# A two-block model forward pass on one core: the first modulation by feature halves, with two of its blocks on TensorE

## What is computed

```
mod = c @ ada_w[l] + ada_b[l]
sh1, sc1, gt1, sh2, sc2, gt2 = [m[:, None, :] for m in jnp.split(mod, 6, axis=-1)]

h = rmsnorm(x, norm1_g[l]) * (1.0 + sc1) + sh1
p = h @ w_in[l]
xr, yr, q, k, v, ga, gb = jnp.split(p, cuts, axis=-1)
...
q = head_rmsnorm(q.reshape(b_, s_, ATT_HEADS, HEAD_DIM), q_norm_g[l])
k = head_rmsnorm(k.reshape(b_, s_, ATT_HEADS, HEAD_DIM), k_norm_g[l])
y_b = stick_breaking_attention(q, k, v)
mix = jax.nn.sigmoid(ga) * y_a + jax.nn.sigmoid(gb) * y_b
x = x + gt1 * (mix @ w_out[l])
```

## Time and profile before

| | us |
|---|---|
| median of 3 runs | 1700.46 (1700.05 to 1700.58) |
| the profiled execution | 1701.61 |
| its span, first to last instruction | 1699.8 |
| TensorE busy in the span | 1653.3 (97%) |
| DVE busy | 988.4 (58%) |
| ScalarE busy | 801.5 (47%) |
| GpSimd busy | 790.1 (46%) |

### The profile page before, as it was taken

One profiled execution on the slowest core, in us unless ns is written; L12 is line 12 of the kernel. 1 busy time (PEld: TensorE's weight loads), 2 busy tenths in 40 slices (PEclk: granted clock), 3 DMA queues, 4 the chain that ended last, 5 costly groups with the idle time before them and its releaser, 6 DMA issues.

```text
span 1699.8 us, 19723 instructions
## 1 busy us (share of the span) xinstructions
PE 1653.3 (97%) x7340; PEld 1347.5 (79%) x7340; DVE 988.4 (58%) x1170; ACT 801.5 (47%) x1005; POOL 790.1 (46%) x577
## 2 busy tenths in 40 slices
PE   4999999999999999999999999999999999999997
PEld 2778887878778888888887888888878888888885
DVE  6676787777837817715642767566446554155541
ACT  2565565666434425514342333677653444244442
POOL 1244443543555545554563544455573342543425
PEclk7999999999999999999999999999999999999999
DMA  9333433242233332333322322211222131331312
GB/s 369 124 124 117 132 109 125 89 136 87 80 101 99 95 101 90 99 124 99 98 89 68 112 84 83 72 42 56 75 87 87 51 99 50 99 99 51 99 50 74
DMA packets 46462, 166.89 MB, mean 98 GB/s; under 512 B 5152, under 2 KB 5280, under 8 KB 45856
## 3 DMA queue, kind: packets, MB, share of 16 engines
q1 hardware_dynamic: 46368, 165.63, 29.8%
HBM read 163.52 MB, written 2.10 MB: 97 GB/s over the span
## 4 chain that ended last, share of the span: by engine, by line
PE 93%; DVE 5%; ACT 1%; DMA 1%; issue 1%; POOL 0%; SPq 0%; POOLq 0%; DVEq 0%; ACTq 0%
PE lin L651 17%; PE lin L653 17%; PE lin L652 17%; PE big L651 7%; PE big L653 7%; PE big L652 7%; DVE scr L1585 1%; PE big L757 1%; PE m_o L777 1%; PE big L1067 1%; PE big L1066 1%; PE big L1065 1%; DMA scr<-ada 1%; PE big L770 1%; PE big L768 1%
## 5 line engine op out<-in xcount | busy, mean ns | idle before, releaser
L617 POOL TENSOR_TENSOR w_lo<-raw,w_hi 128x512 fp32r<-128x512 f32 x200 | 284.4, 1422 | 651.8 <-ACT w_hi L1104 651.7
L651 PE MATMUL lin<-h_hi,w_hi 128*128 128x512 f32 x936 | 368.9, 394 | 2.9 <-POOL w_lo L620 1.8
L653 PE MATMUL lin<-h_hi,w_lo 128*128 128x512 f32 x936 | 365.2, 390 | 0.0
L652 PE MATMUL lin<-h_lo,w_hi 128*128 128x512 f32 x936 | 365.0, 390 | 0.0
L620 POOL TENSOR_TENSOR w_lo<-raw,w_hi 128x512 fp32r<-128x512 f32 x209 | 302.1, 1446 | 14.4 <-ACT w_hi L1104 14.4
L1104 ACT ACTIVATE w_hi<-raw 128x1024 fp32r<-128x1024 f32 (+1 forms) x209 | 217.5, 1041 | 159.4 <-PE m_b L669 50.3
L651 PEld LDWEIGHTS lin<-h_hi,w_hi 128*128 128x128 f32 x936 | 176.1, 188 | 40.7 <-POOL w_lo L620 2.2
L653 PEld LDWEIGHTS lin<-h_hi,w_lo 128*128 128x128 f32 x936 | 176.1, 188 | 37.0
L652 PEld LDWEIGHTS lin<-h_lo,w_hi 128*128 128x128 f32 x936 | 176.2, 188 | 36.6 <-issue 0.7
L617 POOL TENSOR_TENSOR qk_hl<-raw,qk_hl 128x512 fp32r<-128x512 f32 x43 | 60.3, 1402 | 144.2 <-ACT qk_hl L1104 144.1
L651 PE MATMUL lin<-y_hi,w_hi 128*128 128x512 f32 x260 | 101.7, 391 | 1.9 <-DVE y_lo L1749 1.9
(11 more groups left out here) (492 smaller groups left out, 3443.0 us busy)
## 6 DMA issues: line engine op xcount, KB each, us to landing
raw<-weights SPq DMA_DIRECT2D x245, 512.0 KB, 3.6
slab<-ada SPq DMA_DIRECT2D x32, 512.0 KB, 4.4
scr<-ada SPq DMA_DIRECT2D x16, 512.0 KB, 6.3
raw<-weights SPq DMA_DIRECT2D x10, 256.0 KB, 2.7
x<-x_t SPq DMA_DIRECT2D x2, 1024.0 KB, 6.4
out_t<-scr SPq DMA_DIRECT2D x8, 256.0 KB, 2.6
raw<-weights SPq DMA_DIRECT2D x4, 448.0 KB, 3.3
rgw<-rg_w SPq DMA_DIRECT2D x1, 1024.0 KB, 6.6
```

The source lines that it names most:

```text
L617: nc.gpsimd.tensor_tensor(lo[:, 0:4 * P], raw[:, s, 0:4 * P], hi[:, 0:4 * P].bitcast(F32), ALU.subtract).then_inc(w_half, 1)
L651: nc.tensor.matmul(psum_of(n), wh, hi(k), start=(k == 0), stop=False)
L652: nc.tensor.matmul(psum_of(n), wh, lo(k), start=False, stop=False)
L653: last = nc.tensor.matmul(psum_of(n), wl, hi(k), start=False, stop=(k == nk - 1))
```

## The change

- **Halves.** The ada matrix of sh1 and sc1 is laid out anew: blocks 0 to 7 hold sh1 and sc1 for the first 512 features (chunks 0 to 3 of h), blocks 8 to 15 those for chunks 4 to 7. DVE accumulates the first half, starts the second (blocks 8, 9), makes chunks 0 to 3 of h, accumulates blocks 10 to 15, and makes chunks 4 to 7.
- **Two blocks on TensorE.** Blocks 0 and 1 (DIRECT) are not accumulated; sixteen one-column products by the columns of c sum them in m_o, between the fifth and the sixth square of x. DVE adds this to the bias before its last block of the first half. All counts of `ada_used` fall by two.
- **PSUM scratch.** The root stays in m_a, and the gained chunks go to big bank 2 and m_b in turn, not to `rstd` and `tmp`.
- **Units side by side.** `pair` becomes `beside`, with a part of the chunks. Chunks 0 to 3 of q0 and k0, then of v0 and q1; `modulation(1)`; chunks 4 to 7 of q0, k0, v0 together, then of q1, then k1. v0 and q1 use big banks 0 and 1. k1 is cut in three around the head squares. q1 and k1 are then done before the scores of head 0.
- **Copies.** ScalarE copies q0, k0, v0, squares q0, copies q1, squares k0, then splits the weights that `split_ahead(q1)` allows (v1, xr0, yr0), and takes the roots after them.
- **Homes and loads.** The weights of q1 and k1 get homes in free rows of y_hi and y_lo. RING now has the ada blocks 0 to 15 in it, between the weights; `diff`, 448 KB of the constants, is loaded with the gate weights. Some semaphores are joined.

The diff, cut to its core:

```diff
@@ ring_plan
         if h == 0:
-            units += [("q", 0, 8), ("k", 0, 8), ("v", 0, 8), ("ada", a, 8), ("ada", a + 1, 8), ("q", 1, 8),
-                      ("ada", a + 2, 8), ("k", 1, 8), ("ada", a + 3, 8), ("v", 1, 8), ("ada", a + 4, 8)]
+            units += [("ada", i, 8) for i in range(10)] + [("q", 0, 8), ("k", 0, 8), ("ada", 10, 8), ("ada", 11, 8)]
+            units += [("v", 0, 8), ("ada", 12, 8), ("ada", 13, 8), ("q", 1, 8), ("ada", 14, 8), ("ada", 15, 8)]
+            units += [("k", 1, 8), ("ada", a, 8), ("v", 1, 8), ("ada", a + 1, 8)]
             continue
...
+        if h == 1:
+            units += [("ada", a - 2, 8), ("ada", a - 1, 8), ("yr", g, 8), ("ada", a, 8), ("ga", g, 8), ("ada", a + 1, 8),
...
@@ home_plan
-    windows = ((("w_out", 3), ("p_out", 6), None), (("a_out", 0), ("rv", 2), ("qn", HEADS - 1)))
+    windows = ((("w_out", 3), ("p_out", 6), None), (("a_out", 0), ("rv", 2), ("qn", HEADS - 1)),
+               (("q", 0), ("v", 1), None))
@@ SP
-                    sp.wait_ge(ada_used, max(j - NA + 1, ADA_FIRST))
+                    sp.wait_ge(ada_used, max(j - NA + 1, ADA_FIRST) - DIRECT)
@@ PE
             for k in range(DK):
                 square(k + 1, k == 0, k == DK - 1)
+                if k == 4:
+                    direct_blocks()
             modulation(0)
-            modulation(1)
...
                 if h == 0:
-                    pair(("q", 0), ("k", 0), H, L, normed(0))
-                elif h < HEADS:
+                    beside((("q", 0), ("k", 0)), H, L, normed(0), range(4))
+                    beside((("v", 0), ("q", 1)), H, L, normed(0), range(4))
+                    modulation(1)
+                    beside((("q", 0), ("k", 0), ("v", 0)), H, L, normed(0), range(4, DK))
+                    unit("q", 1, H, L, part=range(4, DK))
+                    unit("k", 1, H, L, part=range(4))
+                elif 1 < h < HEADS:
                     unit("q", h, H, L)
                 if h == 1:
-                    unit("k", h, H, L)
+                    pe.wait_ge(v_copied, 1)
+                    pe.wait_ge(q_copied, 2)
...
                 if h == 0:
+                    unit("k", 1, H, L, part=range(4, 6))
                     head_square(2, m_b[:])
+                    unit("k", 1, H, L, part=range(6, DK))
@@ ACT
-            norm_root(square_used, 8, D)
-            split_ahead(0)
-            highs(0)
+            norm_root(square_used, 8, D, m_a[:])
+            split_ahead(0, 1)
+            highs(0, range(2))
+            split_ahead(0, 2)
+            highs(0, range(2, 4))
+            split_ahead(0, 4)
+            highs(0, range(4, DK))
+            for u in range(4):
+                act.wait_ge(unit_done, u + 1)
+                to, signal = ((A(S1["q"], 0), q_copied), (A(S1["k"], 0), k_copied), (V1, v_copied),
+                              (A(S1["q"], 1), q_copied))[u]
+                if u == 3:
+                    head_square(1, A(S1["q"], 0))
+                    act.wait_ge(unit_done, UNIT[("q", 1)] + 1)
+                nc.scalar.activation(to, psum_of(u), ACT.Copy).then_inc(signal, 1)
+            head_square(2, A(S1["k"], 0))
...
+                if h == 0:
+                    split_ahead(UNIT[("q", 1)])
@@ DVE
-            for a in range(ADA_FIRST):
-                accumulate(a)
...
+            for half in range(2):
+                cols = slice(4 * half, 4 * half + 4)
+                for a in range(DIRECT, 10) if half == 0 else range(10, ADA_FIRST):
+                    if a == DK - 1:
+                        dve.wait_ge(direct_done, 1)
...
+                    accumulate(a)
+                dve.wait_ge(mod_done, half + 1)
...
+                        v.scalar_tensor_tensor(out=scaled(0, k), in0=x[:, k], scalar=sm(A1 + k), in1=m_a[:],
+                                               op0=M, op1=M).then_inc(pre_h, 1)
```

More of the change, by code:

```diff
@@ L184, in bank_plan @@
             turn[ring] = 0
-        bank[n] = turn[ring] % ring
-        turn[ring] += 1
+        if (kind, j) in (("v", 0), ("q", 1)):
+            bank[n] = 2 if kind == "v" else 3
+        else:
+            bank[n] = turn[ring] % ring
+            turn[ring] += 1
         before[n] = last.get(bank[n])
@@ L713, in modulation, with beside @@
                 last.then_inc(mod_done, 1)
-            def pair(a, b, hi, lo, ready):
-                na, nb = UNIT[a], UNIT[b]
-                for n in (na, nb):
-                    if BEFORE[n] is not None:
+            def beside(units, hi, lo, ready, part=range(DK)):
+                units = [UNIT[u] for u in units]
+                for n in units:
+                    if BEFORE[n] is not None and part[0] == 0:
                         pe.wait_ge(*freed(n))
-                for k in range(DK):
+                for k in part:
                     pe.wait_ge(*ready(k))
-                    for n in (na, nb):
-                        if k == 0:
+                    for n in units:
+                        if k == part[0]:
                             pe.wait_ge(w_split, PACK[n] + 1)
@@ L732, in pair, with direct_blocks @@
                             last.then_inc(unit_done, 1)
+            def direct_blocks():
+                pe.wait_ge(blocks_loaded, 16 * DIRECT)
+                for m in range(DK):
+                    at = 16 + 8 * (m // 4) + m % 4
+                    for b in range(DIRECT):
+                        last = nc.tensor.matmul(m_o[:, at:at + 1], direct[b][:, m // 4, (m % 4) * P:(m % 4 + 1) * P],
+                                                p_("c", b), start=(b == 0), stop=(b == DIRECT - 1))
+                last.then_inc(direct_done, 1)
             def gained(r):
@@ L1174, in gate, with highs @@
                 act.wait_ge(rgate_done, counted(rgate_done))
-            def highs(r):
-                for k in range(DK):
+            def highs(r, part=range(DK)):
+                for k in part:
                     act.wait_ge(pre_h, DK * r + k + 1)
-                    nc.scalar.activation(h_hi[:, k], tmp[:, k % 4], ACT.Identity,
+                    nc.scalar.activation(h_hi[:, k], scaled(r, k), ACT.Identity,
                                          bias=sm(MOD + 24 * r + k)).then_inc(h_high, 1)
@@ L2312 @@
             home_of[:] = blocks(source(kind, j))
-    ada = i["ada_w"][0].reshape(DK, P, 6, D).transpose(1, 2, 0, 3).reshape(P, NADA, 2, T)
+    ada = i["ada_w"][0].reshape(DK, P, 6, D).transpose(1, 2, 0, 3).reshape(P, 6, DK, 2, T)
+    ada[:, 0:2] = ada[:, 0:2].transpose(0, 3, 2, 1, 4).copy()
+    ada = ada.reshape(P, NADA, 2, T)
     params = np.concatenate([
```

136 lines of the change are left out of this document (85 added, 51 removed).

## The result

| | before | after |
|---|---|---|
| median (lowest to highest), 6 runs each on one chip | 1700.52 us (1699.55 to 1701.47) | 1706.02 us (1704.36 to 1707.81) |
| ratio, 95% interval | | 1.0033 (1.0023 to 1.0042) |
| the profiled execution | 1701.61 us | 1704.36 us |
| its span | 1699.8 us | 1702.4 us |

The change makes the kernel 5.5 us slower. The forecast was 1704.7 us, 4.2 us slower, in a range of 1699.9 to 1708.4. The two marks of the forecast lie at 79.54 us (`scores`, 74.26 before) and 95.95 us (`suffixes`, 91.46 before).

A forecast was written before the change was run, and what follows sets the result against it. TensorE, busy 93%, was taken as the bound, decided before 96 us. Behind by 5.2 us at the scores, 7.3 us with the low clock, 4.2 us at the suffixes after givebacks; added to the median: 1704.7 us, range 1699.9 to 1708.4.

The forecast's parts named there:

- The two marks of the forecast: Starts of the first scores and first suffixes on TensorE; the suffixes' shift was taken as the shift of the end.
- Loads and direct blocks: Start of the kernel: first products end at 25.4 us; two blocks off DVE pay about 1 us, not 2.6 us.
- rival A: Start: the direct products let TensorE's clock fall, first half 3.9 us later, restart 2.2 us later, 1706.9 us; chance 0.22.
- First half of h: h_lo 0 to 3 there at 29.3 to 33.3 us; TensorE works from 31.7 to 44.1, 10.9 us of work.
- Second half, the deciding term: DVE's six remaining accumulations beside five half splits take 12.1 us; TensorE restarts at 51.5, 8.7 us later than before.
- The turns: Second half: DVE accumulations and GpSimd half splits alternate, about 1.1 us each, 12.1 us in all; 7.9 us without.
- rival B: Second half: no turns on DVE, restart at 48.4, 4.0 us less than forecast, 1700.7 us; chance 0.14.
- The scores: First scores: uncovered chain through block 16, yr0's load, splits and roots; TensorE stands 8.1 us, scores at 79.4.
- rival C: First scores: yr0's load is no bound, TensorE stands 4.7 us instead of 8.1, 1701.3 us; chance 0.12.
- D: rival B and rival C together: 7.4 us less than forecast, 1697.3 us; chance 0.10.
- The clock at the scores and what is given back: Low clock adds 2.1 us at scores; a 1.76 us wait and 1.7 us low clock go; suffixes 4.2 us later.
- the step that carries the shift to the end: After 96 us: TensorE is busy to 408 us, so the suffixes' shift, 4.2 us, is the shift of the end.

The follow-up runs named there:

- e4: The changed kernel with no direct blocks on TensorE, all sixteen accumulated on DVE; 1704.62 us, ratio to before 1.0032.
- e3: The changed kernel with k1's weights split after the second half of h, not while DVE accumulates; 1703.8 us, ratio to before 1.0028.
- e1: The changed kernel with the load of yr0 issued ahead of ada block 19; 1701.7 us, ratio to before 1.0012.
- e5: The changed kernel with the edits of e2, e3 and e4 together; 1694.94 us, ratio to before 0.997.
- e7: The changed kernel with the edits of e2 and e3, the two direct blocks left on TensorE; 1696.3 us, ratio to before 0.9979.
- e2: The changed kernel with ScalarE's roots of the head norms ahead of the splits of v1, xr0 and yr0; 1697.51 us, ratio to before 0.9983.
- e8: e5 with head squares and v1's split ahead of q1's copy, plus unread matmuls in TensorE's two idle gaps; 1694.2 us, ratio to before 0.9968.
- e10: e9 plus three unread fp32 products in TensorE's first idle gap; 1691.03 us, ratio to before 0.9946.
- e9: e5 with head squares and v1's split ahead of q1's copy, second modulation products before v0 and q1's last chunk; 1693.77 us, ratio to before 0.9964.

## Why the prediction was right, step by step

**Loads and direct blocks.** DVE's first block came at 13.86 (13.8 was said), it waited 0.36 us for the direct products (0.5), those took 3.63 us (3.4) and ended at 20.65 (20.6), the last squares ended at 23.52 (23.7), the products at 25.19 (25.4). The clock did not fall here, as it would have under rival A. The sentence that the two blocks "pay about 1 us" is wrong all the same, in its sign: e4 has its first products 1.65 us earlier without them, and its whole trace from the suffixes up to 440 us 1.4 us earlier. The working compared the end with the two accumulations' 2.6 us of DVE time and not with when DVE would have been done; it had both numbers for that, 1.27 us a block and 1.32 us an accumulation.

**First half of h.** h_lo 0 to 3 were done at 28.64, 30.22, 31.83 and 32.64, each 0.7 us earlier than said: the operations with one operand in PSUM kept 0.75 us beside half splits of 1.28 us. (The pair shown for it in the earlier trace rows overlapped by 0.4 us only; here it is shown in full.) TensorE began at 28.70 and not at 31.7, since q0's matmuls don't wait for k0's split. It made nothing of that (the burst ended at 43.97, 44.1 was said), because k0's split let it go on at 31.08, and the clock was low until 36.

**Second half, the deciding term.** 12.14 us for six accumulations (12.1), restart at 50.37 (51.5). That is the term that decides, and its size is right. The turns are shown by e3 and e4, and rival B, that the accumulations keep 1.29 us, is refuted. The Trainium skill, GPSIMD Engine Reference, Key points, has the rule that decided between the two readings of the earlier trace rows: DVE contends with GpSimd where it has two SBUF inputs, which fits both the 2.2 us of the accumulations and the 0.75 us of the h operations. The rule gives no price there; here it is 0.9 us for each of the two. The restart came 1.1 us sooner than said. The accumulation began 0.6 us earlier and ended at 44.83 (45.7), 0.9 us earlier: the other 0.3 us is a slip of the sum, since 33.3 and 12.1 make 45.4 and not 45.7. The products were done 2.6 us later (2.6), and the vector and the first h_lo took 2.95 us (3.2).

**The scores.** q1 ended at 63.0 (64.4), and TensorE was ready for the scores at 69.76 (71.3), both by that 1.1 us and a little of the clock. But block 16 was used at 67.83 (68.0), yr0 loaded at 72.84 (73.0), split at 73.97 (74.1), and the scores began at 79.54 (79.4). The matmuls between q1 and the scores hang on nothing in that chain, so a TensorE that got through them sooner only waited longer, 9.78 us in place of 8.1 us. At the head of that chain two errors cancel, by luck: q1 ended 1.4 us sooner, but ScalarE has five passes behind it (3.25 us, to 66.25) where the prediction counted a copy and two more (2.0 us, to 66.4). With one of the two alone the scores would have been missed by some 1.3 us. e1 shows the load as a bound and refutes rival C; with it D falls too. e1 also gives the price of the load: 3.2 us, where C's was 3.4 us.

**The clock at the scores and what is given back.** 2.3 us for the scores at 1.2 GHz (2.1 said), suffixes at 95.95 (95.6), 4.49 us behind before (4.2 said). From 96 to 408 us TensorE was busy throughout and the distance moved by under 0.2 us, as the step that carries the shift to the end had it.

**From the trace to the median.** The shift of the profiled pair up to 440 us is 4.65 us, its spans differ by 2.6 us, and the medians by 5.5 us. The stretches at 1.2 GHz explain the 1.9 us lost between 440 and 504 us in that pair. They lie elsewhere in each execution: e5's and e7's traces differ by 1.7 us at 890 us while they are level at 330. What makes the median 0.9 us larger than the shift at 440 us is open. Executions of one kernel differ by more than that (e1: nine from 1700.8 to 1702.3 us, two at 1705.1 and 1705.5 us), so a median of five or six moves with the few that lie high. In e1 to e4 the differences of the medians to the changed kernel's (4.3, 8.5, 2.2 and 1.4 us, from another series of runs) agree with those of the traces (3.2, 8.4, 1.3 and 1.4 us) to 1.1 us, and no better. That the forecast of the median was met to 1.3 us is therefore weaker evidence than the marks of the trace.

## What to carry to other kernels

Where work is moved ahead of a wait so that an engine has something to do, look at what the moved work covered where it stood: here q1 and k1 hid the head norms. Without their cover, and with the splits ahead of the roots, TensorE stood 9.8 us at the scores and ran them at half clock for 2.3 us more, against the 7.7 us of waits for the accumulations that went; with the roots first the wait is 1.3 us (e2). Then follow each step of the uncovered chain on its engine, with all that stands in the queue ahead of it; three weight splits for later units, one of them behind a load behind a block that DVE had not read, cost 8.4 us, and moving two lines took that away (e2). And an engine that keeps pace with its loads isn't helped by giving some of them to another one.

## What was unexpected of the hardware

- The one-column products with the clock at 2.4 GHz are followed by a fall in some executions and not in others. The windows 20 to 24 us, where squares 6 to 8 stand, of the changed kernel and then of e2, which has the same instructions on TensorE up to there:

```profile
20.00:24.00 4.00, 4.00 (x19) 1.00 1.03 410
```

```profile
20.00:24.00 4.00, 4.00 (x8) 0.60 1.03 410
```

  In e1, e2 and e7 the clock fell behind these products, and the three squares took 4.5, 4.5 and 4.2 us in place of 3.0 us. This is rival A's mechanism. It costs 1.2 to 1.5 us at the squares and not the 3.9 us that the prediction gave it: there the clock stays down to the end of the first products, and here it is up again ahead of them in e1 and e2 (they take 1.84 us, as in the changed kernel) and within them in e7 (2.20 us). In e1 the direct products also began 1.2 us sooner (15.83 against 17.02), since the five squares ahead of them took 6.35 us and not 7.57 us, so its restart was at 50.45 against 50.37. The Trainium skill, TensorE: Matmul & The Clock Gate, Part 1, says that the gate samples activity on a clock of its own, whatever the kernel's start, so that the point of change varies from run to run; that the same instructions met a fall in e2 and none in the changed kernel agrees with it.
- Three fp32 products of 512 columns (2.8 us in e8, 4.5 us in e10) in a gap of 4 us were followed by a burst at 2.4 GHz in the profiled executions of both kernels that had them; the changed kernel, e1 to e7 and e9 ran the stretch from 29 to 33 us at 1.2 GHz.
- DVE and GpSimd side by side are hardly better than one after the other: an accumulation of 1.29 us and a half split of 1.28 us take 2.2 us together, against 2.6 us in sequence.
